# Hyena long convolutions in a hybrid layer: filter tables that swap buffers, filter products split around the inverse transform, spectrum and forward transform woven over four banks

## What is computed

```python
def fft_long_conv(u, kf, bias):
    L = u.shape[1]
    uf = jnp.fft.rfft(u, n=2 * L, axis=1)
    y = jnp.fft.irfft(uf * kf[None], n=2 * L, axis=1)[:, :L]
    return y + u * bias.astype(F32)
...
    kf = hyena_filters(L, lp)
    u3 = short_conv(p[..., COL_HY:COL_GATE], lp['hy_conv_w'], lp['hy_conv_b'], rows).astype(F32)
    v, x1, x2 = jnp.split(u3, 3, axis=-1)
    z2 = x1 * fft_long_conv(v, kf[:, 0], lp['hy_bias'][0])
    y_hy = (x2 * fft_long_conv(z2, kf[:, 1], lp['hy_bias'][1])).astype(dtype)
```

## Time and profile before

| | |
|---|---|
| median of 3 runs | 2294.6 us (2291.41 to 2296.27) |
| the profiled execution, its own time | 2304.29 us |
| its span, first to last instruction | 2302.4 us |
| PE busy | 2174.1 us, 94% |
| DVE busy | 1571.9 us, 68% |
| ACT busy | 1036.6 us, 45% |
| mean granted clock of TensorE | 0.976 of full |
| the projections with the convolutions between them | about 744 to 1282 us of the span |

### The profile page before, as it was taken

The page is one execution under the profiler, slowest core; times in us unless marked ns, Lnnn a source line. Parts: engine busy times, 40 slices in busy tenths (PEclk is TensorE's granted clock), DMA queues, the critical chain, the costliest instruction groups (busy, mean ns, idle before and its releaser), DMA issues. The chain is left out here.

```text
span 2302.4 us, 30766 instructions
## 1 busy us (share of the span) xinstructions
PE 2174.1 (94%) x11866; PEld 1757.2 (76%) x11866; DVE 1571.9 (68%) x2163; ACT 1036.6 (45%) x1353; POOL 114.0 (5%) x133
## 2 busy tenths in 40 slices
PE   4999998999999999999999999998899999999997
PEld 2468886546899877777778999986688888778775
DVE  3347787765654677878776445546677777899997
ACT  4243233123654433333333334444656555677775
POOL 1000000000000002121110100000000000000000
PEclk9999999999999999999999999998999999999998
DMA  9963656887576644343433556643488887999995
GB/s 310 358 196 117 204 166 231 308 329 247 174 233 184 184 123 133 115 133 115 133 115 110 169 160 182 241 152 119 147 263 292 275 277 262 315 361 387 361 340 181
DMA packets 314372, 500.78 MB, mean 218 GB/s; under 512 B 16941, under 2 KB 160904, under 8 KB 313078
## 3 DMA queue, kind: packets, MB, share of 16 engines
q1 hardware_dynamic: 309254, 481.02, 63.0%
q0 software_dynamic: 4976, 17.83, 2.4%
HBM read 496.65 MB, written 2.13 MB: 217 GB/s over the span
## 5 line engine op out<-in xcount | busy, mean ns | idle before, releaser
L187 DVE TENSOR_TENSOR w_lo<-raw,w_hi 128x1024 fp32r<-128x1024 f32 x680 | 824.1, 1237 | 406.0 <-ACT w_hi L183 395.2
L183 ACT ACTIVATE w_hi<-raw 128x1024 fp32r<-128x1024 f32 x680 | 708.9, 1058 | 648.7 <-PE bank L195 471.6
L193 PE MATMUL bank<-h,w_hi 128*128 128x256 f32 (+1 forms) x896 | 296.9, 331 | 10.7 <-DVE w_lo L187 4.3
L194 PE MATMUL bank<-h,w_hi 128*128 128x256 f32 (+1 forms) x896 | 292.1, 326 | 0.0
L195 PE MATMUL bank<-h,w_lo 128*128 128x256 f32 (+1 forms) x896 | 292.1, 326 | 0.0
L1605 PE MATMUL bank<-h,w_hi 128*128 128x512 f32 x768 | 276.7, 404 | 0.0
L1607 PE MATMUL bank<-h,w_lo 128*128 128x256 f32 x768 | 216.4, 282 | 0.0
L193 PEld LDWEIGHTS bank<-h,w_hi 128*128 128x128 f32 x896 | 174.6, 195 | 37.9 <-issue 16.5
L195 PEld LDWEIGHTS bank<-h,w_lo 128*128 128x128 f32 x896 | 174.3, 195 | 13.3
L194 PEld LDWEIGHTS bank<-h,w_hi 128*128 128x128 f32 x896 | 174.5, 195 | 12.8 <-issue 0.5
L1605 PEld LDWEIGHTS bank<-h,w_hi 128*128 128x128 f32 x768 | 145.7, 190 | 38.1 <-issue 3.7
(11 more groups left out here) (456 smaller groups left out, 3705.5 us busy)
## 6 DMA issues: line engine op xcount, KB each, us to landing
raw<-in_w_in SPq DMA_DIRECT2D x240, 512.0 KB, 4.3
raw<-in_ada_w SPq DMA_DIRECT2D x192, 512.0 KB, 6.2
raw<-in_moe_w_gate SPq DMA_DIRECT2D x128, 512.0 KB, 5.3
raw<-in_moe_w_up SPq DMA_DIRECT2D x128, 512.0 KB, 5.7
raw<-in_moe_w_down SPq DMA_DIRECT2D x128, 512.0 KB, 6.0
raw<-in_w_ssd_out SPq DMA_DIRECT2D x32, 512.0 KB, 4.1
raw<-in_w_hy_out SPq DMA_DIRECT2D x32, 512.0 KB, 3.4
raw<-in_w_o SPq DMA_DIRECT2D x32, 512.0 KB, 4.2
```

Of the source, the lines that this page charges most:

```text
L183: act.activation(self.k.w_hi[:, j % HL, :], self.k.raw[:, j % RAW, :], ACT.Copy).then_inc(self.hi_ready, 1)
L187: dve.tensor_tensor(self.k.w_lo[:, j % HL, :], self.k.raw[:, j % RAW, :], self.k.w_hi[:, j % HL, :].bitcast(F32), ALU.subtract).then_inc(s ...
L193: pe.matmul(out, lhs[0], rhs[0], start=start, stop=False)
L194: pe.matmul(out, lhs[0], rhs[1], start=False, stop=False)
```

## The change

Four edits in this stage, none in the others.

1. `hs` and `ktab` swap roles with every convolution: `own_of(n)` and `other_of(n)` give the table that holds filters, taps and product of convolution `n`, and the one for the absolute values, the half-way butterflies and the spectrum. With that, `decayed(n)` no longer waits for the inverse transform of convolution n-1 to have read `hs`; the wait goes to `absolute(n)` on ACT.
2. `filters(n)` is cut in two halves. For n = 1 to 7 the first stands before the inverse transform of convolution n-1, the second behind it; `decayed` is cut alike, the first half ahead of `scaled`.
3. `spectrum` and `forward` become `transforms`, which weaves their eight products.
4. `turn(2*i)` moves on PE from behind projection `6*i+4` to behind projection `6*i+5`, just ahead of `norms(2*i)`. The loop of ACT, and with it the place of `keep_turned(2*i)`, stays as it is.

```diff
+        def own_of(n):
+            return (hs, ktab)[n % 2]
+        def other_of(n):
+            return (ktab, hs)[n % 2]
...
-                def filters(n):
+                def filters(n, half):
...
                     if n:
                         pe.wait_ge(s.prod, n)
-                    for m in range(4):
+                    for m in (2 * half, 2 * half + 1):
                         if m >= 2:
                             pe.wait_ge(s.hmul, 4 * n + m - 1)
...
-                def spectrum(n):
+                def transforms(n):
                     pe.wait_ge(s.bfly, n + 1)
-                    for m in range(4):
-                        if m >= 2:
-                            pe.wait_ge(s.kcopy, 4 * n + m - 1)
-                        pe.matmul(k.psum[6 + m % 2][:], spec[:, m, :], hs[:, m, :], start=True,
-                                  stop=True).then_inc(s.kmm, 1)
+                    pe.wait_ge(s.tcopied, n + 1)
+                    for what, m in (("s", 0), ("s", 1), ("f", 0), ("s", 2), ("f", 1), ("s", 3), ("f", 2), ("f", 3)):
+                        if what == "s":
+                            if m >= 2:
+                                pe.wait_ge(s.kcopy, 4 * n + m - 1)
+                            pe.matmul(k.psum[6 + m % 2][:], spec[:, m, :], own_of(n)[:, m, :], start=True,
+                                      stop=True).then_inc(s.kmm, 1)
+                        else:
+                            if m >= 2:
+                                pe.wait_ge(s.kcopy, 4 * n + m + 1)
+                            mm = pe.matmul(k.psum[4 + m][:], fwd[:, m, :], tok[:, m // 2, :], start=True, stop=True)
+                    mm.then_inc(s.umm, 1)
...
-                def forward(n):
-                    pe.wait_ge(s.tcopied, n + 1)
-                    pe.wait_ge(s.kcopy, 4 * n + 4)
-                    for m in range(4):
-                        mm = pe.matmul(k.psum[4 + m][:], fwd[:, m, :], tok[:, m // 2, :], start=True, stop=True)
-                    mm.then_inc(s.umm, 1)
...
                         if i and pp == 0:
-                            spectrum(first)
-                            forward(first)
+                            transforms(first)
                         if i and pp == 1:
+                            filters(second, 0)
                             inverse(first)
-                            filters(second)
+                            filters(second, 1)
                         if i and pp == 2:
                             turn(second)
                             norms(second)
                         if i and pp == 3:
-                            spectrum(second)
-                            forward(second)
+                            transforms(second)
+                        if i < 4 and pp == 4:
+                            filters(2 * i, 0)
                         if i and pp == 4:
                             inverse(second)
                         if i < 4 and pp == 4:
-                            filters(2 * i)
+                            filters(2 * i, 1)
+                        if i < 4 and pp == 5:
                             turn(2 * i)
-                        if i < 4 and pp == 5:
                             norms(2 * i)
...
                 def absolute(n):
                     act.wait_ge(s.hmul, 4 * n + 4)
-                    act.activation(ktab[:], hs[:], ACT.Abs).then_inc(s.nabs, 1)
+                    if n:
+                        act.wait_ge(s.vmm, n)
+                    act.activation(other_of(n)[:], own_of(n)[:], ACT.Abs).then_inc(s.nabs, 1)
...
-                def decayed(n):
-                    if n % 2 == 0:
+                def decayed(n, half):
+                    if n % 2 == 0 and half == 0:
                         dve.wait_ge(s.decay, 16 * (n // 2) + 16)
-                    if n:
-                        dve.wait_ge(s.vmm, n)
-                    for m in range(4):
+                    for m in (2 * half, 2 * half + 1):
                         dve.wait_ge(s.hgen, 4 * n + m + 1)
...
                         splits(b)
+                        if i < 4 and pp == 5:
+                            decayed(2 * i, 0)
                         if i and pp == 5:
                             scaled(second, x2).then_inc(s.full, 1)
                         if i < 4 and pp == 5:
-                            decayed(2 * i)
+                            decayed(2 * i, 1)
...
                         if i and pp == 2:
+                            decayed(second, 0)
                             scaled(first, x1).then_inc(s.z2, 1)
-                            decayed(second)
+                            decayed(second, 1)
```

More of the change, by code:

```diff
@@ L1503, in absolute_sum @@
                 def absolute_sum(n):
+                    mag = other_of(n)
                     pool.wait_ge(s.nabs, n + 1)
-                    pool.tensor_tensor(ktab[:, 0:2, :], ktab[:, 0:2, :], ktab[:, 2:4, :], ALU.add).then_inc(s.pool, 1)
+                    pool.tensor_tensor(mag[:, 0:2, :], mag[:, 0:2, :], mag[:, 2:4, :], ALU.add).then_inc(s.pool, 1)
                     pool.wait_ge(s.pool, n + 1)
-                    pool.tensor_tensor(ktab[:, 0, :], ktab[:, 0, :], ktab[:, 1, :], ALU.add).then_inc(s.nadd, 1)
+                    pool.tensor_tensor(mag[:, 0, :], mag[:, 0, :], mag[:, 1, :], ALU.add).then_inc(s.nadd, 1)
                 load_filter(0)
@@ L1631, in norms @@
                 def norms(n):
+                    mag = other_of(n)
                     pe.wait_ge(s.nadd, n + 1)
-                    pe.matmul(k.psum[6][0:1, :], k.ones[:, 0:1], ktab[:, 0, :], start=True, stop=True)
+                    pe.matmul(k.psum[6][0:1, :], k.ones[:, 0:1], mag[:, 0, :], start=True, stop=True)
                     for c in range(4):
-                        mm = pe.matmul(k.psum[7][:, c:c + 1], ktab[:, 0, c * P:(c + 1) * P], k.ones[:, 0:1],
+                        mm = pe.matmul(k.psum[7][:, c:c + 1], mag[:, 0, c * P:(c + 1) * P], k.ones[:, 0:1],
                                        start=True, stop=True)
                     mm.then_inc(s.nsum, 1)
-                def spectrum(n):
+                def transforms(n):
                     pe.wait_ge(s.bfly, n + 1)
-                    for m in range(4):
-                        if m >= 2:
-                            pe.wait_ge(s.kcopy, 4 * n + m - 1)
-                        pe.matmul(k.psum[6 + m % 2][:], spec[:, m, :], hs[:, m, :], start=True,
-                                  stop=True).then_inc(s.kmm, 1)
+                    pe.wait_ge(s.tcopied, n + 1)
[10 more added lines that the diff above has]
+                    mm.then_inc(s.umm, 1)
                 def turn(n):
@@ L1668, in inverse @@
                             mm = pe.matmul(k.psum[4 + c // 2][:, (c % 2) * L:(c % 2 + 1) * L],
-                                           hs[:, f, c * P:(c + 1) * P], idft[:, f, :], start=(f == 0), stop=(f == 3))
+                                           own_of(n)[:, f, c * P:(c + 1) * P], idft[:, f, :], start=(f == 0), stop=(f == 3))
                     mm.then_inc(s.vmm, 1)
@@ L1782, in keep_spectrum @@
                         act.wait_ge(s.kmm, 4 * n + m + 1)
-                        act.activation(ktab[:, m, :], k.psum[6 + m % 2][:], ACT.Copy).then_inc(s.kcopy, 1)
+                        act.activation(other_of(n)[:, m, :], k.psum[6 + m % 2][:], ACT.Copy).then_inc(s.kcopy, 1)
                 def keep_turned(n):
@@ L1921, in merge @@
                     dve.tensor_tensor(m, m, v[:, 2 * (g % 2):2 * (g % 2) + 2, :], ALU.mult).then_inc(s.merged, 1)
-                def decayed(n):
-                    if n % 2 == 0:
+                def decayed(n, half):
+                    if n % 2 == 0 and half == 0:
                         dve.wait_ge(s.decay, 16 * (n // 2) + 16)
-                    if n:
-                        dve.wait_ge(s.vmm, n)
-                    for m in range(4):
+                    for m in (2 * half, 2 * half + 1):
                         dve.wait_ge(s.hgen, 4 * n + m + 1)
-                        dve.tensor_tensor(hs[:, m, :], k.psum[6 + m % 2][:], decay[:, m, :],
+                        dve.tensor_tensor(own_of(n)[:, m, :], k.psum[6 + m % 2][:], decay[:, m, :],
                                           ALU.mult).then_inc(s.hmul, 1)
@@ L1937, in taps @@
                 def taps(n):
+                    taps_, mid = own_of(n), other_of(n)
                     dve.wait_ge(s.nsum, n + 1)
@@ L1942, in taps @@
                     dve.wait_ge(own.sem, own.at())
[L1943 to L1947, removed]
+                    own.own(dve, dve.tensor_tensor(taps_[0:1, 0, :], taps_[0:1, 0, :], brow[:], ALU.add))
+                    own.inc(dve.tensor_tensor(mid[:, 0:2, :], taps_[:, 0::2, :], taps_[:, 1::2, :], ALU.add))
+                    own.own(dve, dve.tensor_tensor(mid[:, 2:4, :], taps_[:, 0::2, :], taps_[:, 1::2, :], ALU.subtract))
```

(7 more changed lines are left out.)

## The result

The changed kernel takes 2277.57 us (median of 6, 2276.67 to 2281.07), the kernel before beside it 2295.81 us (median of 6): a ratio of 0.9918, 95% interval 0.9901 to 0.9934, so 15 to 23 us, 18 by the medians. It is faster by clearly more than 0.2%, and 2279 was forecast. The profiled execution has a span of 2279.0 us.

A forecast was written before the change was run, and what follows sets the result against it. PE was taken to bound the stage, busy 86.2 of 90 us, with about 22 us idle to be had. Terms -12.0 - 15.9 + 12.0 = -15.9 us took the 2294.6 us median to 2279; range 2271 to 2288.

The forecast's parts named there:

- weave, 8 times: Spectrum and forward products on PE: weaving them closes gaps of 1.5 us in each of eight convolutions, 12.0 us saved.
- halves, 7 times: At seven filters, two pairs cost 1.8 (up to 2.3) instead of 4.07 us: 15.9 us saved, 12.7 at other bound.
- turn, 4 times: ACT's copy holds back four splits; PE waits 1.8 and 1.1 us, together 3.0 per turn, 12.0 lost over four.
- the rival in which DVE is late: Filters: DVE reaches the first half late, the wait moves behind the inverse transform; gain only 7.5 us, 2287; chance 0.12.
- S: End of projection 11 on PE; forecast: PE goes on at S + 4.5, table of taps ready at S + 17.0.
- stall two: Spectrum after projections 6, 12, 18, 24: PE waits 1.1 us for the table of taps.
- The rival of the half clock behind the turn: Clock falls to half after turn, norms and idle PE; net 0.6 to 1.9 us per turn, 2281 to 2286; chance 0.15.
- the forecast's own signs of being wrong: `w_lo` and `taps` waits absent, either above 3 us, clock falling behind all four turns, or a new PE wait for DVE.
- the fall of the clock at all four turns: Sign against the forecast: half clock on PE behind each of the four moved turns.
- the missing wait for `taps`: Sign against the forecast: no 1.1 us wait of the spectrum for `taps`; absence was named jointly with the `w_lo` wait's.

The follow-up runs named there:

- weave only: Kernel before with the woven spectrum and forward products alone; median 2273.3 us, ratio to before 0.987.
- halves only: Kernel before with swapped tables and halved filters alone, turn at its old place, spectrum and forward not woven; median 2282.4 us, ratio 0.9914.
- copy behind: Changed kernel with ACT's copy of the turned input behind the four splits of projection 6i+6 instead of ahead; median 2268.8 us, ratio to before 0.9848.
- turn only: Kernel before with the moved turn of even convolutions alone; median 2310.2 us, ratio to before 1.0038.
- filler run: Changed kernel with two dense products, result unused, behind the norms of convolutions 0, 2, 4, 6; median 2280.1 us, ratio to before 0.9923.

## Why the prediction was right

Its steps, with what the stage shows for each:

| term | forecast | measured |
|---|---|---|
| weave, 8 times | -12.0 | -14.0 (weave only, without the fall) |
| halves, 7 times | -15.9, bound -12.7 | -12.6 (halves only, without fall and turn waits) |
| turn, 4 times | +12.0 | +12.0 (changed against copy behind), +12.9 (turn only) |
| sum | -15.9 | -14.8 (changed against before), -13.4 without the fall |

- *The weave* was mis-sized by 2 us. A pass costs 0.43 us (945.16 to 948.59 holds eight passes), not 0.45, so more of the old block was gap; and the last forward product does not wait visibly for the last copy.
- *The halves* came out at the other bound. A pair costs 1.06 us, near its modelled 1.13, and I had taken 0.9; two pairs in place of 4.07 us save 1.95, and the inverse transform behind the first pair takes 0.1 more than it did. The mechanism held in every filter, and the rival in which DVE is late did not occur.
- *The turn* was right as a mechanism and in its sum: ACT in program order, first split at S + 2.0, PE at S + 4.5, table at S + 17.0. One step of it failed: stall two did not appear as a wait of 1.1 us. The rival of the half clock behind the turn occurred, at four turns of four, with 1.5 us each (12.9 instead of 11.4); but its stretch lies over the wait for the table, so together they cost 1.5, not 2.6. The prediction had said that overlap (it subtracted the 1.1), and had given the rival 0.15 and a net price of 0.6 to 1.9 us per turn; 0.2 (the filler run) to 0.4 (1.5 less 1.1) came. Of the forecast's own signs of being wrong one was met in full, the fall of the clock at all four turns, and one by half, the missing wait for `taps`, although the sum was hardly moved by them. The filler run shows both sides: without the half clock the wait is there.
- *The total.* The terms measured apart make 14.6 us, 1.2 more than the 13.4 of all together. The stage gives 14.8 us against one profile of before and 21.1 against the other, since the halved clock behind the filter gaps strikes there once or five times, and the changed kernel has no such gaps. The measured 18 lies between. That the halves also remove these falls was in no term of the sum; the prediction named it only as an argument against its half-clock rival. So it is in part luck that the forecast lies within 2 us of the median: the halves were overvalued by 3 us, and less half clock, inside and outside the stage, which no term held, made up for it.

The Trainium skill, page "TensorE: Matmul & The Clock Gate" (section "Why this matters for your kernels"), puts the return of the slow clock down to idle gaps between bursts of matmuls. These runs agree in kind, and add that the same gap of 1.29 us was followed by it between no time and five times in seven. The same page of the Trainium skill (section "Architectural detail: the array is 16x 32x32, not 1x 128x128") says that ScalarE's queue is strictly first in, first out. The trace agrees: four splits, whose buffers PE freed one by one during projection 11, all stood behind the copy until it had run, after 8.63 us of idle ACT.

The scatter of 1800 to 1817 us outside the stage, in unchanged code, goes with its time at half clock, 65 to 98 us. What stays open is what sets that amount, and so why the weave's whole time is 30 us below before and not 14.

## What to carry to other kernels

When a producer is moved in the order of one engine, look for its consumer in the order of every other: an in-order engine that works one round ahead will stop there with a full round of its own work behind the consumer. A gain and a loss of this kind can stand in one change; moving the ACT copy too took 12 us more from the same stage. Read small changes by the length of their stage in the profile, start to start, and count the stretches of half clock in it before comparing; for whole times, put the mean granted clock of the executions beside them.

## What the runs showed of the hardware

The half clock is not a fixed price of a given gap. Seven equal gaps of 1.29 us were followed by it not at all, once, once and five times in four profiles; turn, norms and 1.54 us of idle time, eight times out of eight in two kernels; turn and norms with no idle time behind them, at none of twelve even convolutions in the three kernels that had it so, nor at any odd convolution. The cases within a profile are not independent: the even turns of the changed kernel start 108.8 to 109.2 us apart and the falls behind them at the same distance, so the eight are two observations of a repeating pattern. Each fall was a stretch of a little over 3 us at 1.2 GHz and cost 1.4 to 1.6 us, unless something else was late behind it: there it cost 0.2 us, the difference between the changed kernel and the one with the filler, per turn.
